# Hybrid RWKV-7 / Hyena block on one Trainium2 core: column picks on TensorE and token mixing on VectorE in the first stage, and Hyena products on VectorE with closing banks one after the other

## Chip, core and metric

The kernel runs on 1 core of one Trainium2 chip. The metric is the device time of one execution in microseconds (us), the median of several runs. The notes below name five engines: PE (TensorE), DVE (VectorE), ACT (ScalarE), POOL (GpSimd) and SP (SyncE, which here only issues DMAs).

## What is computed

Two layers over 256 latent tokens (and 256 context tokens in layer 0), width 1024, all in float32. Layer 0 mixes tokens by a bidirectional RWKV-7, layer 1 by an order-2 Hyena; each is followed by a mixture of 32 experts, top 2. Cut to what the change touches:

```python
# layer 0, the inputs of the RWKV mixer, for latent and context tokens
hx = rms_norm(x, g) * (1.0 + sc1x) + sh1x        # sc, sh: columns of cond @ ada_w + ada_b
xx = 0.5 * (prev(hx) + next(hx)) - hx
xr, xw, xk, xv, xa, xg = (hx + xx * mix[n] for n in range(6))
# low-rank products: tanh(xw @ w1), xa @ a1, sigmoid(xg @ g1)

# layer 1, Hyena: two long convolutions by Fourier products, then a projection
def _fft_conv(u, kern, skip):
    y = irfft(rfft(u) * rfft(kern))[:, :L]
    return y + u * skip
z = x1 * _fft_conv(v, kern[:, 0], skip[0])
y = x2 * _fft_conv(z, kern[:, 1], skip[1])
ox = y @ w_out + b_out
x = x + g1x * ox
```

## The kernel before

The kernel is a sequence of blocks with a barrier of all engines between them: `rwkv_inputs`, `rwkv_heads`, experts of layer 0, `hyena_inputs`, `hyena_convolutions`, experts of layer 1, `final_norm`. Inside a block each engine follows its own list in program order, and semaphores tie the lists together. The change touches the first block and `hyena_convolutions`.

**`rwkv_inputs`.** Channels lie on partitions, in 8 tiles `t` (KT = 8); `hT` holds the transposed normalized tokens (context and latent side by side, 2 x 256 columns for each tile) and `xx` the shifted difference. `FirstModulation` computes shift and scale: `products` sums cond x ada_w in one PSUM bank as the 8 weight tiles arrive, `add_bias` (L179, DVE) writes the result as a row, `columns` (L151) turns that row into columns by partition with 8 small DMAs that ACT issues, and `wait_columns` makes DVE wait for all of them. Then DVE forms `sc` and `edge` (L474 to L477), and a loop over the 8 tiles scales `hT` on DVE (L484) and `xx` on ACT (L397) and signals `tile_ready`. PE follows it tile by tile with the products for `w` (L426, L427), and after them those for `a` (L432) and `g` (L437, L439). The mixed tokens come from `mix_tokens` (L345): DVE forms a, g, k and r, 8 instructions each, with one signal `mixed` at the end of each name; POOL forms v with 8 multiplications (L503) and 8 additions (L506).

**`hyena_convolutions`.** For each of two orders `od`: PE transposes `u` and applies the forward transform to half 0 of the channels, then half 1 (L2643), ACT copies the spectra out as `vhat` (L2682). DVE forms the real part of the product with the filter spectrum (L2704, L2705, L2707), POOL the imaginary part (L2691, L2692, L2694), each in three instructions over 128x1024. PE then runs the inverse transform (L2654) over the 8 channel tiles `m`; for each half it waits for both parts before its first product. DVE closes each `m` with three instructions: `u * skip` (L2712), the transform times norm plus that (L2714), and the gate (L2717 or L2719). After order 1 PE multiplies by `w_out` (L2666) into four PSUM banks, with `m` outside and the banks inside, so that all four end in the last `m`; DVE adds bias, multiplies by the gate row and adds to `x_res`, three instructions for each bank (L2728, L2730, L2732). SP waits for `y_done` 8 (the end of the inverse transform of order 1) before it loads the first `up` and `down` weights of layer 1's experts.

**What follows.** The experts of layer 1 load 16 pairs of experts through rings of buffers; each load waits until PE has finished with the buffer.

Of the kernel before, what the change touches and what calls it, by code (L numbers as in the profile page):

```python
# [17 lines left out]
ALU = mybir.AluOpType  # L18
# [3 lines left out]
P = 128  # L22
D = 1024
L = 256
# [88 lines left out]
class FirstModulation:  # L113
# [4 lines left out]
    def __init__(self, s, ins, low, scale, shift):  # L118

        self.s, self.ins, self.scale, self.shift = s, ins, scale, shift  # L120
        self.raw, self.sig, self.cond = s.take(2, KT), s.take(2, KT), s.take(KT, 32)
        self.w = [low[:, t * FIRST:(t + 1) * FIRST] for t in range(6)] + [s.take(FIRST) for _ in range(KT - 6)]
        self.bias, self.row = s.take(512), s.take(512)
        self.cond_in, self.sig_done, self.cond_ready = s.sem("cond_in"), s.sem("cond_sig"), s.sem("cond_ready")
        self.ada_in = [s.sem(f"ada_in{t}") for t in range(KT)]
        self.bias_in, self.sum_done, self.row_ready, self.cols_in = (s.sem(n) for n in ("ada_b_in", "ada_sum", "ada_row", "ada_cols"))

    def load_conditions(self, sp):
        sp.dma_start(self.raw[:, 0], self.ins["c"].rearrange("b (p t) -> p (b t)", t=KT)).then_inc(self.cond_in, 16)
        sp.dma_start(self.raw[:, 1], self.ins["c_ctx"].rearrange("(p t) -> p t", t=KT)).then_inc(self.cond_in, 16)  # L130

# [13 lines left out]

    def columns(self, act):
        act.wait_ge(self.row_ready, 1)
        for q in range(self.PARTS):
            dst = (self.shift, self.scale)[q // 2]
            for i in range(2):  # L150
                act.dma_start(dst[q % 2 * 64:q % 2 * 64 + 64, 1 - i, :],  # L151
                              self.row[q * 32 + i:q * 32 + i + 1, :].rearrange("o (p t) -> o p t", t=KT)).then_inc(self.cols_in, 16)

    def wait_columns(self, dve):
        dve.wait_ge(self.cols_in, self.PARTS * 2 * 16)

# [12 lines left out]
    def conditions(self, dve):  # L169
        dve.memset(self.cond, 0.0)  # L170
        dve.drain()
        dve.wait_ge(self.sig_done, 1)
        dve.tensor_tensor(self.s.cond, self.raw[:, 0], self.sig[:, 0], ALU.mult)
        dve.tensor_tensor(self.cond[:, :, 0:2].rearrange("p t i -> p i t"), self.raw, self.sig, ALU.mult).then_inc(self.cond_ready, 1)
# [121 lines left out]
def rwkv_inputs(s, r, ins):  # L296
# [34 lines left out]
    def both(v):  # L331
        return v.rearrange("p (i c) -> p i c", i=2)
# [4 lines left out]
    def mix_tokens(dve, name):  # L337

        k = which[name]
        for t in range(KT):  # L340
            if name in "rg":
                args = (dst[name][:, t], xx[:, t * 2 + 1], mix[:, k, t:t + 1], hT[:, t * 2 + 1, 1:L + 1])
            else:
                args = (both(dst[name][:, t]), xx[:, t * 2:t * 2 + 2], mix[:, k, t:t + 1], inner(t))
            op = dve.scalar_tensor_tensor(*args, ALU.mult, ALU.add)  # L345
        return op

    tiles = [(ctxn, 0), (ctxn, 1), (s.x_res, 0), (s.x_res, 1)]

    with nc.Block(name="rwkv_inputs", no_gpsimd_drain=True) as block:  # L350
# [17 lines left out]
        def _(act):  # L368
# [38 lines left out]
        def _(pe):  # L407
# [6 lines left out]
            for t in turn_order:  # L414
# [14 lines left out]
            pe.wait_ge(a_in, 32)  # L429
            pe.wait_ge(mixed, 1)  # L430
            for t in range(KT):
                mm = pe.matmul(s.psum[3][:, :], a1[:, t].rearrange("p a b -> p (a b)"), xa[:, t], start=(t == 0), stop=(t == KT - 1))  # L432
            mm.then_inc(lora_done, 1)
            pe.wait_ge(g_in, 16)
            pe.wait_ge(mixed, 2)
            for t in range(KT):
                pe.matmul(s.psum[4][:, 0:L], g1[:, t, 0:P], xg[:, t], start=(t == 0), stop=(t == KT - 1))  # L437
            for t in range(KT):
# [4 lines left out]
        def _(dve):  # L443
# [29 lines left out]
            first.wait_columns(dve)  # L473
            dve.tensor_scalar(sc, sc, 1.0, None, ALU.add)  # L474
            dve.tensor_scalar(edge, sh.rearrange("p i t -> p t i"), -0.5, None, ALU.mult)
            dve.drain()
            dve.tensor_tensor(sc, sc, ng.unsqueeze(1).to_broadcast([P, 2, KT]), ALU.mult)  # L477
            dve.drain()
            dve.sem_inc(scale_ready, 1)
            ends = xx.rearrange("p a b -> p a b")  # L480
            for t in range(KT):
# [7 lines left out]
                dve.sem_inc(tile_ready, 1)  # L489
            for name in ("a", "g", "k", "r"):  # L490
                mix_tokens(dve, name).then_inc(mixed, 1)

        @block.gpsimd
        def _(pool):
# [4 lines left out]
            pool.sem_inc(folded, 1)  # L499
            pool.wait_ge(tile_ready, KT)  # L500
            to = lambda t: both(r.xv[:, t])
# [5 lines left out]
            pool.drain()  # L507

# [1769 lines left out]
def hyena_layer(s, hy, experts, ins, mods):  # L2278
# [66 lines left out]
    with nc.Block(name="hyena_inputs", no_gpsimd_drain=True) as block:  # L2345
# [263 lines left out]
        ("vT_done", "vt_ready", "dft_done", "vhat_ready", "real_ready", "imag_ready", "y_done", "y_ready"))  # L2609
    o_done = S("o_done")  # L2610
    with nc.Block(name="hyena_convolutions", no_gpsimd_drain=True) as block:
# [15 lines left out]
        def _(pe):  # L2627
            for od in range(2):
# [17 lines left out]

                for m in range(CH):
                    if m % 4 == 0:
                        pe.wait_ge(real_ready, od * 2 + m // 4 + 1)
                        pe.wait_ge(imag_ready, od * 2 + m // 4 + 1)  # L2650
                    k = 0
                    for part in range(2):
                        for ft in range(2):
                            mm = pe.matmul(s.psum[m // 2][:, m % 2 * L:(m % 2 + 1) * L], prod[:, part, ft, m * P:(m + 1) * P], inv[part][:, ft],  # L2654
                                           start=(k == 0), stop=(k == 3))
                            k += 1
                    if m % 2:
                        mm.then_inc(y_done, 1)
            pe.wait_ge(vhat_ready, 16)
            for m in range(CH):  # L2660
                pe.wait_ge(y_ready, 9 + m)
                if m % 4 == 0:
                    pe.wait_ge(wout_in[m // 4], 16)
                for i in range(TT):
                    for h in range(2):
                        mm = pe.matmul(s.psum[4 + i * 2 + h][:, :], u[:, CH + m, i * P:(i + 1) * P], w_out[:, m, h * 512:(h + 1) * 512],  # L2666
                                       start=(m == 0), stop=(m == CH - 1))
                        if m == CH - 1:
                            mm.then_inc(o_done, 1)

        @block.scalar
        def _(act):
            for od in range(2):
                for half in range(2):
# [9 lines left out]
        @block.gpsimd  # L2684
        def _(pool):

            for od in range(2):
                for half in range(2):
                    c = slice(half * 512, (half + 1) * 512)
                    pool.wait_ge(vhat_ready, (od * 2 + half) * 4 + 4)  # L2690
                    pool.tensor_tensor(prod[:, 1, :, c], vhat[:, 0, :, c], khat[:, od, 1, :, c], ALU.mult)  # L2691
                    pool.tensor_tensor(half_b, vhat[:, 1, :, c], khat[:, od, 0, :, c], ALU.mult)  # L2692
                    pool.drain()
                    pool.tensor_tensor(prod[:, 1, :, c], prod[:, 1, :, c], half_b, ALU.add).then_inc(imag_ready, 1)  # L2694
                    pool.drain()

        @block.vector
        def _(dve):
            for od in range(2):

                for half in range(2):
# [4 lines left out]
                    dve.drain()  # L2706
                    dve.tensor_tensor(prod[:, 0, :, c], prod[:, 0, :, c], half_a, ALU.subtract).then_inc(real_ready, 1)  # L2707
                    dve.drain()

                for m in range(CH):  # L2710
                    dve.wait_ge(y_done, od * 4 + m // 2 + 1)
                    dve.tensor_scalar(u[:, m], u[:, m], skip[:, od * CH + m:od * CH + m + 1], None, ALU.mult)  # L2712
                    dve.drain()
                    dve.scalar_tensor_tensor(u[:, m], s.psum[m // 2][:, m % 2 * L:(m % 2 + 1) * L], norm[:, od * CH + m:od * CH + m + 1], u[:, m], ALU.mult, ALU.add)  # L2714
# [99 lines left out]
```

## Time and profile before

| quantity | value |
|---|---|
| runs | 2031.36, 2028.88, 2026.99 us; median 2028.88 |
| profiled execution | 2029.0 us, its span 2027.2 us |
| mean granted TensorE clock | 0.949 |
| PE, DVE, ACT, POOL busy | 88%, 39%, 26%, 9% of the span |
| `rwkv_inputs` | from 0 to about 81.4 us |
| `hyena_convolutions` | from about 1402.5 to 1512.4 us |

All positions below are us from the start of the span. The shares of busy time are means over stages with different limits; what a change inside one block is worth is read from the chain of waits inside that block, and then from whether the blocks behind it start their own work relative to its end.

### The profile page before, as it was taken

The page shows a single profiled execution, that of the slowest core. Times are in us where ns is not written, and L with a number is a line of the kernel's source. Part 1 is how long each engine was busy: PE and PEld are TensorE (multiplying, and loading weights), DVE is VectorE, ACT ScalarE, POOL GpSimd, SP SyncE. Part 2 cuts the span into 40 slices and gives each one's busy share as a digit, 9 for nine tenths or more (in the row PEclk, how much of TensorE's full clock was granted, in tenths as well). Part 3 has the DMA queues.
Part 4 walks back from the last instruction along what each step waited for, and adds up shares of the span by engine and source line. Part 5 has one row for each costly group of instructions (what it writes and reads, how often), then busy time and mean ns, then how long its engine had stood idle before and what let it go on. Part 6 is the DMA issues. An engine that isn't in the chain of part 4 may idle for free. (4 is left out here: it accounts for less than half of the span.)

```text
span 2027.2 us, 34188 instructions
## 1 busy us (share of the span) xinstructions
PE 1778.4 (88%) x13907; PEld 951.2 (47%) x13907; DVE 787.7 (39%) x1857; ACT 534.6 (26%) x985; POOL 179.2 (9%) x121
## 2 busy tenths in 40 slices
PE   3868888887887897999999999798887999999996
PEld 1435545455545545444344443575545434443442
DVE  4766675666676534411011000574844301100101
ACT  2244543544544412111111111313111111111111
POOL 1512102102112000000000000000600000000000
PEclk8879998999989897999999999899997999999998
DMA  9012322323323447999999998233154999999993
GB/s 298 0 57 80 99 84 84 104 80 100 102 82 101 155 137 314 423 428 429 428 428 428 429 428 313 84 125 119 69 221 190 422 428 428 428 428 429 429 410 126
DMA packets 105808, 504.06 MB, mean 249 GB/s; under 512 B 16208, under 2 KB 60992, under 8 KB 79824
## 3 DMA queue, kind: packets, MB, share of 16 engines
q1 hardware_dynamic: 103728, 501.88, 62.4%
q8 instruction: 90, 1.47, 0.3%
q10 hardware_dynamic: 1952, 0.39, 0.1%
q14 instruction: 38, 0.31, 0.0%
HBM read 501.13 MB, written 1.09 MB: 248 GB/s over the span
## 5 line engine op out<-in xcount | busy, mean ns | idle before, releaser
L2005 DVE TENSOR_TENSOR arena<-banks,arena 128x512 f32<-128x512 f32 x32 | 22.1, 692 | 661.0 <-PE banks L1820 661.0
L1820 PE MATMUL banks<-arena 128*64 128x512 f32 x1024 | 226.3, 594 | 11.1 <-DMA arena<-in_moe_w_up 11.1
L1842 PE MATMUL banks<-arena 128*64 128x512 f32 x1024 | 226.8, 595 | 3.3 <-ACT arena L1936 3.3
L1811 PE MATMUL banks<-arena 128*64 128x512 f32 x1024 | 225.3, 592 | 3.3 <-DVE arena L1928 3.3
L800 PE MATMUL banks<-arena 128*128 128x512 f32 (+1 forms) x384 | 158.6, 550 | 0.8 <-ACT arena L1109 0.8
L1820 PEld LDWEIGHTS banks<-arena 128*64 128x64 f32 x1024 | 82.1, 137 | 153.7 <-issue 153.7
L1811 PEld LDWEIGHTS banks<-arena 128*64 128x64 f32 x1024 | 74.3, 137 | 147.8 <-issue 144.2
L1842 PEld LDWEIGHTS banks<-arena 128*64 128x64 f32 x1024 | 70.7, 137 | 154.5 <-issue 150.7
L1930 ACT ACTIVATE arena<-banks,arena 128x128 f32<-128x128 f32 x128 | 48.2, 457 | 341.4 <-PE banks L1800 341.4
L1800 PEld LDWEIGHTS banks<-arena 128*128 128x128 f32 x1024 | 121.8, 199 | 28.1 <-issue 24.3
L1800 PE MATMUL banks<-arena 128*128 128x128 f32 x1024 | 127.9, 285 | 3.5 <-DVE arena L2000 3.5
L1849 PE MATMUL banks<-arena 128*128 128x512 f32 x256 | 115.4, 593 | 2.4 <-ACT arena L1941 2.4
L2194 POOL TENSOR_TENSOR x_res<-x_res,arena 128x512 f32<-128x512 f32 x8 | 9.9, 1263 | 1106.0 <-DVEq L2170 566.5
L800 PEld LDWEIGHTS banks<-arena 128*128 128x128 f32 x384 | 69.5, 194 | 60.1 <-issue 51.1
L1940 ACT ACTIVATE arena<-banks 128x512 f32<-128x512 f32 x32 | 19.1, 597 | 282.5 <-PE banks L1842 282.5
L2424 PE MATMUL banks<-arena 128*128 128x256 f32 x384 | 87.4, 386 | 0.0
L1928 DVE TENSOR_SCALAR arena<-banks,arena 128x128 f32<-128x128 f32 x128 | 43.7, 403 | 100.8 <-PE banks L1800 100.8
L2424 PEld LDWEIGHTS banks<-arena 128*128 128x128 f32 x384 | 73.4, 193 | 17.0 <-issue 6.9
L1849 PEld LDWEIGHTS banks<-arena 128*128 128x128 f32 x256 | 46.1, 190 | 50.0 <-issue 45.9
L228 PE MATMUL banks<-arena 128*32 128x384 f32 (+1 forms) x384 | 50.0, 595 | 16.8 <-DMA arena<-in_ada_w 12.2
L1921 ACT ACTIVATE arena<-banks 128x512 f32<-128x512 f32 x32 | 19.1, 597 | 169.7 <-PE banks L1811 169.7
L737 POOL TENSOR_TENSOR arena<-arena,const 128x512 f32<-128x512 f32 x16 | 20.4, 1276 | 435.4 <-PE banks L911 421.0
(393 smaller groups left out, 2550.2 us busy)
## 6 DMA issues: line engine op xcount, KB each, us to landing
arena<-in_moe_w_gate SPq DMA_DIRECT2D x64, 2048.0 KB, 14.9
arena<-in_moe_w_up SPq DMA_DIRECT2D x64, 2048.0 KB, 17.1
arena<-in_moe_w_down SPq DMA_DIRECT2D x64, 2048.0 KB, 13.5
arena<-in_ada_w SPq DMA_DIRECT2D x128, 192.0 KB, 2.9
arena<-in_ada_w SPq DMA_DIRECT2D x64, 256.0 KB, 3.5
arena<-in_rw_wrkv SPq DMA_DIRECT2D x24, 512.0 KB, 5.1
arena<-in_hy_w_in SPq DMA_DIRECT2D x6, 2048.0 KB, 8.8
arena<-in_ada_w SPq DMA_DIRECT2D x8, 1024.0 KB, 17.1
```

The costliest lines, as they stand in the source:

```text
L228: mm = pe.matmul(bank[g * 32:(g + 1) * 32, 0:self.width(piece)], self.cond[:, half * self.HALF + g], self.w[g][:, 0:self.width(piece)], st ...
L737: pool.tensor_tensor(M1, src, mask("lev1", BLK), ALU.mult)
L800: mm = pe.matmul(s.psum[OPEN.bank(n, name)][:, 0:width], wkv[k][:, t], x[:, t], start=(t == 0), stop=(t == KT - 1))
L1800: mm = pe.matmul((X0, X1)[k // 4][:, k % 4 * P:(k % 4 + 1) * P], hx[:, t, k * P:(k + 1) * P], sel[par][:, t].rearrange("p a b -> p (a b)") ...
L1811: mm = pe.matmul(G[j * CAP:(j + 1) * CAP, :], xT[:, t, j * CAP:(j + 1) * CAP], wg[par][j][:, t], start=(t == 0), stop=(t == KT - 1))
L1820: mm = pe.matmul(U[j * CAP:(j + 1) * CAP, :], xT[:, t, j * CAP:(j + 1) * CAP], wu[j][:, t], start=(t == 0), stop=(t == KT - 1))
L1842: mm = pe.matmul(bank[j * CAP:(j + 1) * CAP, :], hT[:, t, j * CAP:(j + 1) * CAP], wd[j][:, t, half * 512:(half + 1) * 512], start=(t == 0) ...
L1849: pe.matmul(OUT[k][:, :], selwT[par][:, k // 2], y[:, k % 2 * 512:(k % 2 + 1) * 512], start=start, stop=stop).then_inc(scat_done, 1)
L1928: op = eng.tensor_scalar(xT[:, k], src, sc[:, k:k + 1], sh[:, k:k + 1], ALU.mult, ALU.add)
L1930: op = eng.activation(xT[:, k], src, ACT.Identity, bias=sh[:, k:k + 1], scale=sc[:, k:k + 1])
L2005: dve.tensor_tensor(h, U[:, :], sg, ALU.mult).then_inc(h_ready, 1)
L2424: mm = pe.matmul(s.psum[n % 2][:, 0:L], win_ring[k][:, t, q * P:(q + 1) * P], hT[:, t], start=(t == 0), stop=(t == KT - 1))
```

## The change

In the first block the shift and scale columns come from TensorE: 16 products with columns of the identity pick the row's entries into partitions (bank 5), and DVE reads them from PSUM. The context's condition takes slot 0 and the latent's slot 1, so that the columns come out in order. The last difference on `xx` is split into three quarters, `add_bias`, and one quarter. POOL's mixing for v goes to DVE, between k and r, and every mixing instruction signals `mixed`, so that PE takes `a` and `g` by the tile.

In `hyena_convolutions` DVE forms both parts of the products and POOL nothing. The inverse transform runs by half, then by part, so that the real part's products need only `real_ready`. `u * skip` goes to ACT. The output projection runs `m` = 0 to 3 as before and then bank by bank over `m` = 4 to 7, each bank with its own `o_done`.

```diff
+    def columns(self, pe, bank):
+        pick = self.s.c("ident").rearrange("p (a h r) -> p h a r", a=2, h=2)
+        pe.wait_ge(self.row_ready, 1)
+        for t in range(KT):
+            for h in range(2):
+                mm = pe.matmul(bank[h * 64:(h + 1) * 64, t * 4:(t + 1) * 4], self.row[:, t::KT], pick[:, h, :, 0:2], start=True, stop=True)
+        mm.then_inc(self.cols_done, 1)
+    def take_columns(self, dve, bank, gain, edge):
+        cols = bank[:, 0:KT * 4].rearrange("p (t a i) -> p t a i", a=2, i=2)
+        dve.wait_ge(self.cols_done, 1)
+        dve.scalar_tensor_tensor(self.scale.rearrange("p i t -> p t i"), cols[:, :, 1], 1.0,
+                                 gain.unsqueeze(2).to_broadcast([P, KT, 2]), ALU.add, ALU.mult)
+        dve.tensor_copy(self.shift.rearrange("p i t -> p t i"), cols[:, :, 0])
+        dve.tensor_scalar(edge, cols[:, :, 0], -0.5, None, ALU.mult)
...
-            first.columns(act)
...
             first.products(pe, s.psum[0], range(2, KT))
+            pe.wait_ge(raw_act, 3)
+            first.columns(pe, s.psum[5])
...
-            first.add_bias(dve, s.psum[0])
-            dve.scalar_tensor_tensor(xx, xx, 0.5, hT[:, :, 1:L + 1], ALU.mult, ALU.subtract)
+            for at in (slice(0, 3 * KT // 2), slice(3 * KT // 2, 2 * KT)):
+                if at.start:
+                    first.add_bias(dve, s.psum[0])
+                dve.scalar_tensor_tensor(xx[:, at], xx[:, at], 0.5, hT[:, at, 1:L + 1], ALU.mult, ALU.subtract)
...
-            for name in ("a", "g", "k", "r"):
-                mix_tokens(dve, name).then_inc(mixed, 1)
+            for name in ("a", "g", "k", "v", "r"):
+                mix_tokens(dve, name)
...
-            for t in range(KT):
-                pool.tensor_scalar(to(t), xx[:, t * 2:t * 2 + 2], mix[:, which["v"], t:t + 1], None, ALU.mult)
-            pool.drain()
-            for t in range(KT):
-                pool.tensor_tensor(to(t), to(t), inner(t), ALU.add)
...
+                for half in range(2):
                     for part in range(2):
+                        pe.wait_ge((real_ready, imag_ready)[part], od * 2 + half + 1)
+                        for m in range(4 * half, 4 * half + 4):
+                            for ft in range(2):
+                                mm = pe.matmul(...)
+                            if part == 1 and m % 2:
+                                mm.then_inc(y_done, 1)
...
+            for k in range(4):
+                for m in range(CH // 2, CH):
+                    if k == 0:
+                        pe.wait_ge(y_ready, 9 + m)
+                    mm = out_product(m, k)
+                mm.then_inc(o_done, 1)
...
+                for m in range(CH):
+                    act.activation(u[:, m], u[:, m], ACT.Copy, scale=skip[:, od * CH + m:od * CH + m + 1]).then_inc(skip_ready, 1)
...
                     dve.tensor_tensor(prod[:, 0, :, c], prod[:, 0, :, c], half_a, ALU.subtract).then_inc(real_ready, 1)
+                    dve.tensor_tensor(prod[:, 1, :, c], vhat[:, 0, :, c], khat[:, od, 1, :, c], ALU.mult)
+                    dve.tensor_tensor(half_b, vhat[:, 1, :, c], khat[:, od, 0, :, c], ALU.mult)
+                    dve.drain()
+                    dve.tensor_tensor(prod[:, 1, :, c], prod[:, 1, :, c], half_b, ALU.add).then_inc(imag_ready, 1)
...
-                    dve.tensor_scalar(u[:, m], u[:, m], skip[:, od * CH + m:od * CH + m + 1], None, ALU.mult)
-                    dve.drain()
+                    dve.wait_ge(skip_ready, od * CH + m + 1)
```

## Rows read from the trace of the kernel before

**Rows 1.** Page, busy us, share of the span and instructions.

```profile
PE 1778.4 (88%) x13907; PEld 951.2 (47%) x13907; DVE 787.7 (39%) x1857; ACT 534.6 (26%) x985; POOL 179.2 (9%) x121
```

**Rows 2.** Windows: length, then busy us of each engine, clock, DMA share, GB/s.

```profile
1510.00:1560.00 50.00, 37.61 (x181) 28.33 (x182) 21.87 (x97) 13.93 (x22) 0.00 (x0) 0.69 0.38 150
1600.00:1700.00 100.00, 98.71 (x486) 42.31 (x484) 8.45 (x21) 16.10 (x32) 0.00 (x0) 1.00 1.01 427
```

**Rows 3.** Timeline of PE late in layer 1's experts: start, length, instruction, wait.

```profile
1900.54 7.09 PE L1820 MATMUL banks<-arena 128*64 128x512 f32 x32 [0.49 <-DMA arena<-in_moe_w_up]
...
1929.91 7.09 PE L1820 MATMUL banks<-arena 128*64 128x512 f32 x32 [0.50 <-DMA arena<-in_moe_w_up]
```

**Rows 4.** Timeline of the first block and the start of the second.

```profile
27.58 4.42 DVE L466 TENSOR_TENSOR arena<-arena 128x4096 f32<-128x4096 f32 x1
...
34.16 0.69 DVE L179 TENSOR_TENSOR arena<-banks,arena 128x512 f32<-128x512 f32 x1 [2.16 <-PE banks L163]
...
45.38 0.17 DVE L474 TENSOR_SCALAR arena<-arena 128x16 f32<-128x16 f32 x1 [6.20 <-DMA arena<-arena]
...
46.01 6.49 ACT L397 ACTIVATE arena<-arena 128x256 f32<-128x256 f32 x16 [19.06 <-DVEq L478]
...
47.30 2.05 PE L426 MATMUL banks<-arena 128*128 128x512 f32 x2 [13.28 <-DVEq L488]
...
53.80 27.57 DVE L345 SCALAR_TENSOR_TENSOR arena<-arena 128x512 f32<-128x512 f32 x32
...
76.58 0.38 ACT L403 ACTIVATE arena<-banks 128x256 f32<-128x256 f32 x1 [5.14 <-PE banks L439]
...
83.81 2.08 PE L791 MATMUL banks<-arena 64*128 64x512 f32 x4 [7.27 <-DVEq L1541]
```

**Rows 5.** Line L345 in 54.5 to 56, and in 80.3 to 81.4: ns min/median/max.

```profile
L345 DVE SCALAR_TENSOR_TENSOR arena<-arena x3: 741/750/1096, 53.8 to 55.5; 128x512 f32<-128x512 f32 x3
...
L345 DVE SCALAR_TENSOR_TENSOR arena<-arena x2: 470/470/471, 80.5 to 80.9; 128x256 f32<-128x256 f32 x2
```

**Rows 6.** Timeline of the Hyena products, order 0.

```profile
1414.66 1.23 DVE L2704 TENSOR_TENSOR arena<-arena 128x1024 f32<-128x1024 f32 x1 [12.48 <-ACT arena L2682]
...
1415.80 3.37 DVE L2705 TENSOR_TENSOR arena<-arena 128x1024 f32<-128x1024 f32 x1
...
1423.46 2.29 DVE L2704 TENSOR_TENSOR arena<-arena 128x1024 f32<-128x1024 f32 x1 [0.99 <-ACT arena L2682]
1424.81 8.83 PE L2654 MATMUL banks<-arena 128*128 128x256 f32 x32 [2.02 <-POOL arena L2694]
...
1434.67 7.14 PE L2654 MATMUL banks<-arena 128*128 128x256 f32 x32 [1.03 <-POOL arena L2694]
1434.75 0.48 DVE L2714 SCALAR_TENSOR_TENSOR arena<-banks,arena 128x256 f32<-128x256 f32 x1
1435.31 0.42 DVE L2717 TENSOR_TENSOR arena<-arena 128x256 f32<-128x256 f32 x1
1435.65 0.35 DVE L2712 TENSOR_SCALAR arena<-arena 128x256 f32<-128x256 f32 x1
```

**Rows 7.** Timeline of order 1's end, the projection, and the next block.

```profile
1461.38 7.14 PE L2654 MATMUL banks<-arena 128*128 128x256 f32 x32 [2.02 <-POOL arena L2694]
...
1471.24 7.14 PE L2654 MATMUL banks<-arena 128*128 128x256 f32 x32 [2.72 <-POOL arena L2694]
...
1478.22 27.63 PE L2666 MATMUL banks<-arena 128*128 128x512 f32 x64
...
1503.39 0.69 DVE L2728 TENSOR_TENSOR arena<-banks,arena 128x512 f32<-128x512 f32 x1 [21.82 <-PE banks L2666]
...
1512.74 3.65 PE L1858 MATMUL banks<-const,x_res 128*128 128x128 f32 x16 [6.89 <-PEq L2611]
```

**Rows 8.** Timeline: the same router product in layer 0 and in layer 1.

```profile
773.89 1.95 PE L1864 MATMUL banks<-arena 128*128 128x36 f32 x16 [0.46 <-DVE arena L2026]
...
1516.64 3.60 PE L1864 MATMUL banks<-arena 128*128 128x36 f32 x16 [0.25 <-DVE arena L2026]
```

More of the change, by code:

```diff
@@ L125, in __init__ @@
         self.ada_in = [s.sem(f"ada_in{t}") for t in range(KT)]
[L126 removed]
+        self.bias_in, self.sum_done, self.row_ready, self.cols_done = (s.sem(n) for n in ("ada_b_in", "ada_sum", "ada_row", "ada_cols"))
     def load_conditions(self, sp):
[L129 to L130 removed]
+        sp.dma_start(self.raw[:, 1], self.ins["c"].rearrange("b (p t) -> p (b t)", t=KT)).then_inc(self.cond_in, 16)
+        sp.dma_start(self.raw[:, 0], self.ins["c_ctx"].rearrange("(p t) -> p t", t=KT)).then_inc(self.cond_in, 16)
     def load_bias(self, act):
@@ L144, in sigmoid @@
         act.activation(self.sig, self.raw, ACT.Sigmoid).then_inc(self.sig_done, 1)
[L146 to L155, printed above, removed]
+    def columns(self, pe, bank):
[12 more added lines that the diff above has]
+        dve.tensor_scalar(edge, cols[:, :, 0], -0.5, None, ALU.mult)
     def products(self, pe, bank, tiles):
@@ L344, in mix_tokens @@
                 args = (both(dst[name][:, t]), xx[:, t * 2:t * 2 + 2], mix[:, k, t:t + 1], inner(t))
-            op = dve.scalar_tensor_tensor(*args, ALU.mult, ALU.add)
-        return op
+            dve.scalar_tensor_tensor(*args, ALU.mult, ALU.add).then_inc(mixed, 1)
     tiles = [(ctxn, 0), (ctxn, 1), (s.x_res, 0), (s.x_res, 1)]
@@ L429, in _ @@
             pe.wait_ge(a_in, 32)
-            pe.wait_ge(mixed, 1)
             for t in range(KT):
+                pe.wait_ge(mixed, t + 1)
                 mm = pe.matmul(s.psum[3][:, :], a1[:, t].rearrange("p a b -> p (a b)"), xa[:, t], start=(t == 0), stop=(t == KT - 1))
@@ L434, in _ @@
             pe.wait_ge(g_in, 16)
-            pe.wait_ge(mixed, 2)
             for t in range(KT):
+                pe.wait_ge(mixed, KT + t + 1)
                 pe.matmul(s.psum[4][:, 0:L], g1[:, t, 0:P], xg[:, t], start=(t == 0), stop=(t == KT - 1))
@@ L472, in _ @@
             dve.wait_ge(vec_in, 2 * 16)
-            first.wait_columns(dve)
-            dve.tensor_scalar(sc, sc, 1.0, None, ALU.add)
-            dve.tensor_scalar(edge, sh.rearrange("p i t -> p t i"), -0.5, None, ALU.mult)
-            dve.drain()
-            dve.tensor_tensor(sc, sc, ng.unsqueeze(1).to_broadcast([P, 2, KT]), ALU.mult)
+            first.take_columns(dve, s.psum[5], ng, edge)
             dve.drain()
@@ L2609, in hyena_layer @@
         ("vT_done", "vt_ready", "dft_done", "vhat_ready", "real_ready", "imag_ready", "y_done", "y_ready"))
-    o_done = S("o_done")
+    o_done, skip_ready = S("o_done"), S("skip_ready")
     with nc.Block(name="hyena_convolutions", no_gpsimd_drain=True) as block:
@@ L2645, in _ @@
                         mm.then_inc(dft_done, 1)
[L2647 to L2651, printed above, removed]
-                    for part in range(2):
[L2653 to L2658, printed above, removed]
+                for half in range(2):
+                    for part in range(2):
+                        pe.wait_ge((real_ready, imag_ready)[part], od * 2 + half + 1)
+                        for m in range(4 * half, 4 * half + 4):
+                            for ft in range(2):
+                                mm = pe.matmul(s.psum[m // 2][:, m % 2 * L:(m % 2 + 1) * L], prod[:, part, ft, m * P:(m + 1) * P], inv[part][:, ft],
+                                               start=(m % 2 == 0 and part == 0 and ft == 0), stop=(m % 2 == 1 and part == 1 and ft == 1))
+                            if part == 1 and m % 2:
+                                mm.then_inc(y_done, 1)
@@ L2659, in _, with out_product @@
+            def out_product(m, k):
+                i, h = divmod(k, 2)
+                return pe.matmul(s.psum[4 + k][:, :], u[:, CH + m, i * P:(i + 1) * P], w_out[:, m, h * 512:(h + 1) * 512],
+                                 start=(m == 0), stop=(m == CH - 1))
             pe.wait_ge(vhat_ready, 16)
-            for m in range(CH):
+            for m in range(CH // 2):
                 pe.wait_ge(y_ready, 9 + m)
[L2662 to L2669, printed above, removed]
+                if m == 0:
+                    pe.wait_ge(wout_in[0], 16)
+                for k in range(4):
+                    out_product(m, k)
@@ L2671, in _ @@
+            pe.wait_ge(wout_in[1], 16)
+            for k in range(4):
+                for m in range(CH // 2, CH):
[3 more added lines that the diff above has]
+                mm.then_inc(o_done, 1)
         @block.scalar
```

17 lines of the change are left out of this document (1 added, 16 removed).

## The prediction

> **What bounds the kernel now.** I read the page first. TensorE is busy 88% of the span and VectorE 39% [rows 1], so on average neither of the touched engines (VectorE, GpSimd) is the limit, and a change to them can only pay inside the two blocks it edits, where barriers make a late engine everybody's. So the second thing to ask is whether the blocks behind pass a shift on. The windows show the experts of layer 1 with PE at 98.7% and the DMA engines full at 427 GB/s [rows 2], and late in them PE waits a little at every pair for the `up` weights, at a period of 1929.91 - 1900.54 = 29.37 us [rows 3]: that is the weight stream's period. It is a stream that PE starts: each load waits for a buffer that PE frees, and in 1510 to 1560 the DMA engines are busy only 38% of the time [rows 2], which is some 31 us of slack in front of it. An earlier end of `hyena_convolutions` should therefore arrive at the end of the kernel in full. The heads block, too, starts its loads and products relative to its own barrier, so the same is expected of the first block.
>
> Third, the timeline of the two blocks. In the first the row of shift and scale is there at 34.85, and VectorE goes on only at 45.38, after a wait for the column DMAs [rows 4]. The tile loop runs 46.01 to 53.80. Then VectorE mixes for 27.57 us and ends the block at 81.37; TensorE and ScalarE are through at about 77.2 (L403 at 76.58, and the short one behind it), so VectorE closes the block by 4 us [rows 4]. In the Hyena block TensorE waits for GpSimd's imaginary part in front of each of the four halves: 2.02, 1.03, 2.02, 2.72 us [rows 6, 7].
>
> **What mixing and products cost without GpSimd.** The 128x1024 product takes 1.23 us when it starts ahead of GpSimd's, and 3.37 us for the next of the same shape, with GpSimd's beside it [rows 6]. L345 shows the same: 128x512 takes 741 ns at the best and 1096 at the worst within 1.5 us, and 128x256 takes 470 ns once GpSimd is done [rows 5]. So the two engines hold each other up, and the sum uses the low values. For a pitch from start to start: L466 has 4096 elements in 4.42 us, and the two last 256-element instructions start 0.40 apart (80.5 to 80.9) [rows 4, 5]. A line through both gives 1.04 ns for an element and 0.13 us fixed, so 0.67 us for 512; the product of 1024 has a pitch of 1.14 (1414.66 to 1415.80) [rows 6].
>
> The Trainium skill (SBUF — State Buffer, section on the two separate sides) says that VectorE, when it reads two SBUF inputs, and GpSimd take one port pair as an exclusive lock for a whole instruction, and that the loser blocks. By that rule the long values are waiting and not work, which agrees with the 1.23 beside 3.37; without it the slow rival below would have to get a larger chance. The trace shows it only where both engines run, and only for two or three instructions the free price.
>
> **First block, part by part.** (1) L466 ends at 32.0. Three quarters of the difference are 3072 elements, 3.3 us, to 35.4; then `add_bias`, 0.69, to 36.1. That is 1.3 us later than before, because `sum_done` at about 34.0 now waits behind the 3.3 us. (2) The picks: 16 products, which the trace will show as 32, as it does for float32. Not in the trace before. Nearest is L1864, 16 instructions with 128-column weights and 36 moving columns in 1.95 us at full clock and 3.60 at half [rows 8], so 0.11 and 0.22 each. The picks have 64 columns of weights: below, half of 0.11, so 1.8 us in all; above, the whole 0.22, so 7 us. TensorE has then been idle for 2 us and may be at either clock; I take 3.0. (3) `take_columns` and drains, 0.8 us, against 0.6 before. Tile loop from about 40.0 in place of 46.0: 6.0 earlier. (4) Tile loop unchanged, 7.8 us, to 47.9. (5) VectorE mixes 24 of 512 and 16 of 256: 24 x 0.67 + 16 x 0.40 = 22.5 us, to 70.4. (6) TensorE and ScalarE: from the first L426 at 47.30 to the end of ScalarE at 77.2 is 29.9 us of products that wait only for tiles that come in time (`a` is mixed by 53.3, needed at about 56.5; `g` by 56.5, needed at 63.4). Moved to 41.3 they end at 71.2. So TensorE is the next to be late: the block ends at 71.2 and not at 70.4, and the gain is 81.4 - 71.2 = 10.1 us. Taking a and g by the tile costs and gains nothing, since TensorE is still in the `w` products; if that cover were gone the wait would be 5 us. The column DMAs leave ACT's queue, behind which nothing but the scaling stood. The 40 signals are not in the trace: I take nothing for them; even 0.02 us each would stay in the 0.8 us that VectorE is ahead.
>
> **Hyena block.** Half 0 of order 0: VectorE from 1414.66, six instructions and two drains at 1.14 to 1.23, real part ready at 1418.3, imaginary at 1421.9. Half 1's spectra come at 1423.4 [rows 6]: real at 1427.1, imaginary at 1430.8 (before: 1434.5). TensorE ends its forward transforms at 1422.8 and goes straight on: 32 instructions at 0.217 are 6.95 us, to 1429.7, half 1's real part to 1433.1 and the imaginary to 1436.6; nothing is waited for, with 2.4 us to spare at the tightest place. Before it was 1434.67 + 6.9 = 1441.6. Of the 5.0 us, 2.0 and 1.0 are the waits, 1.7 the clock dip in 8.83 against 7.14 [rows 6], the rest the gap. Order 1: the same waits again, 2.0 and 2.7, together 4.7 [rows 7], and no dip to save; sum 9.7, and with rounding of ends 9.9. `u * skip` on ScalarE: 8 x 0.41 (L397: 16 in 6.49 us) behind its last copy, done at 1426.8, 4 us before VectorE asks; if that cover were gone it would cost 3.3 us per order. Closings: per `m` 0.56 + 0.34 = 0.90 us in place of 0.90 + 0.42 [rows 6]; they are covered by TensorE's next transforms before as after.
>
> Projection: the same 64 instructions, 27.6 us, from 1468.3 to 1495.9. Before, the first bank came 24.9 us into it and VectorE needed four times three instructions, to 1512.37 [rows 7]; now three banks are closed while TensorE works and the last takes 0.1 + 0.76 + 0.76 + 0.69 = 2.3 us, to 1498.1. After TensorE's end 6.5 us become 2.3: 4.3 less. Sum of the block: 9.9 + 4.3 = 14.2 us. The first `up` and `down` loads leave 10 us earlier, the next gate loads 14 us earlier; PE wants them some 50 us after, so they cost nothing.
>
> **Sum.** 10.1 + 14.2 = 24.3 us. There is also the clock: TensorE starts the heads block and the router after shorter idle times (3 us in place of 7.27 and 2.7 in place of 6.89 [rows 4, 7]). The three router products in a row would take 1.95 in place of 3.60 each, up to 4.8 us [rows 8]; in the heads block 2.08 + 9.30 us of products at mostly half clock hide up to 2.7. Idle times of 2 to 3 us in this trace were sometimes followed by the half clock (the 8.83) and sometimes not (7.14 after 2.02 and 2.72 us of waiting) [rows 6, 7]. I count 1 us of these 7.5. So the profiled 2029.0 (span 2027.2, and 1.8 around it) becomes 2029.0 - 25.3 = 2003.7. The median of the runs, 2028.88, is the same number within 0.1.
>
> **Rivals.**
> - The clock stays up in both places: 2029.0 - 24.3 - 7.5 = 1997.2. For it, the shorter idle; against it, the 8.83. Chance 0.15 for more than half of it.
> - A new wait in the first block: picks at the upper bound (7 us), 4 later, or TensorE colder in the `w` products. 2008 to 2010. Chance 0.12.
> - Part of the gain is absorbed: the weight stream of layer 1 cannot start earlier, and Hyena's 14.2 are lost, 2018; or the heads block loses the 10.1, 2014. Against it, the 38% [rows 2]. Chance 0.06.
> - The other sign: the 3.3 us are VectorE's own price for such a product and 1.23 the exception. Then 12 products in a row for each order take 39.6 us: order 0 ends at 1414.66 + 39.6 + 3.5 = 1457.8, 16.3 later than before, both orders 32 later, less 4.3; the first block mixes 27.57 + 8 x 1.01 = 35.7 us and ends at 83.5, 2 later. Together 30 slower, 2059. It starts to be slower than before where the product costs over 2.5 us: 2 x (12p - 23.3) = 14.4. Chance 0.03.
> - It does not do what it says: no engine is freed because TensorE is the bound in both blocks anyway; 2025 to 2033. Against it the four waits for POOL. Chance 0.03.
>
> The forecast has the remaining 0.61 (2001 to 2008). The range that leaves out two in ten reaches into the clock's case and over the first block's: 1997 to 2011. A measurement of this kernel can tell some 0.2%, 4 us: faster by more 0.94, within 0.03, slower 0.03.
>
> **What would show it.** Right: L2704 to L2707 and the three behind them all at 1.15 to 1.25 us; TensorE without a wait over 0.3 us in front of the inverse transforms; `w_out` products from about 1458 (1468 less the first block's 10); L345 at 0.74 and 0.47, 40 of them; the first L426 about 6 us earlier; the block's last work on ScalarE. Wrong: a wait of VectorE for `skip_ready`; L345 over 0.9 us; picks that last over 5 us; waits for `in_moe_w_up` that appear in the first pairs of layer 1.

## The result, and the profile after

The changed kernel takes 2001.05 us (median of 4 runs, 1998.48 to 2007.12) against 2027.93 for the kernel before (4 runs, 2024.94 to 2031.36); ratio 0.987, 95% interval 0.9846 to 0.9895. By that ratio it is 26.4 us less (21 to 31); between the two medians it is 26.9. The forecast was 2003.7 from 2029.0, 25.3 less. The profiled execution is the slowest of the four, 2007.12 with a span of 2005.2 us, so it shows only 22.0 us of the gain; where the rest lies is a question of its own below.

The page's engine line, beside [rows 1]: GpSimd's 68.6 us have gone, and VectorE, which took over that work, is busy 18 us less.

```profile
PE 1776.6 (89%) x13939; PEld 949.0 (47%) x13939; DVE 769.8 (38%) x1862; ACT 541.1 (27%) x1001; POOL 110.6 (6%) x93
```

The timeline of the first block, beside [rows 4]:

```profile
32.01 3.36 DVE L477 SCALAR_TENSOR_TENSOR arena<-arena 128x3072 f32<-128x3072 f32 x1
...
35.28 0.68 DVE L185 TENSOR_TENSOR arena<-banks,arena 128x512 f32<-128x512 f32 x1
35.41 1.90 POOL L501 TENSOR_TENSOR arena<-arena 128x1024 f32<-128x1024 f32 x1 [35.00 <-DMA arena<-in_rw_w]
...
35.88 2.51 DVE L477 SCALAR_TENSOR_TENSOR arena<-arena 128x1024 f32<-128x1024 f32 x1
...
36.11 2.09 PE L152 MATMUL banks<-const,arena 128*64 128x4 f32 x32 [2.07 <-DVE arena L185]
...
38.58 0.18 DVE L158 SCALAR_TENSOR_TENSOR arena<-banks,arena 128x16 f32<-128x16 f32 x1 [0.19 <-issue]
...
40.33 2.05 PE L432 MATMUL banks<-arena 128*128 128x512 f32 x2 [2.12 <-DVEq L492]
...
57.17 3.17 PE L438 MATMUL banks<-arena 128*128 128x512 f32 x7
...
71.26 0.38 ACT L407 ACTIVATE arena<-banks 128x256 f32<-128x256 f32 x1 [5.14 <-PE banks L445]
...
72.31 0.17 DVE L1527 MEMSET arena<- 128x128 f32 x1 [3.15 <-PEq L355]
...
74.29 2.08 PE L787 MATMUL banks<-arena 64*128 64x512 f32 x4 [3.07 <-DVEq L1537]
```

The wait for the column DMAs is gone: VectorE takes the columns at 38.58 where it stood until 45.38. VectorE is idle for 3.15 us before the barrier, so TensorE and ScalarE now end the block, and the next block's first product starts at 74.29 in place of 83.81.

The timeline of the Hyena products, beside [rows 6]. GpSimd is absent, each product takes 1.22 or 1.23 us, and one row of 64 instructions on TensorE has taken the place of two with waits between them:

```profile
1411.12 1.22 DVE L2695 TENSOR_TENSOR arena<-arena 128x1024 f32<-128x1024 f32 x1 [11.54 <-ACT arena L2684]
...
1412.26 1.22 DVE L2696 TENSOR_TENSOR arena<-arena 128x1024 f32<-128x1024 f32 x1
...
1419.09 13.98 PE L2648 MATMUL banks<-arena 128*128 128x256 f32 x64
...
1419.92 1.23 DVE L2695 TENSOR_TENSOR arena<-arena 128x1024 f32<-128x1024 f32 x1 [1.57 <-ACT arena L2684]
...
1425.92 1.23 DVE L2702 TENSOR_TENSOR arena<-arena 128x1024 f32<-128x1024 f32 x1
```

The projection and the block's end, beside [rows 7]. Three banks close inside the projection; after the last one VectorE has one bank left, and TensorE's idle time in front of the router is 2.63 us in place of 6.89:

```profile
1464.26 27.63 PE L2655 MATMUL banks<-arena 128*128 128x512 f32 x64
...
1481.70 0.69 DVE L2722 TENSOR_TENSOR arena<-banks,arena 128x512 f32<-128x512 f32 x1 [15.29 <-PE banks L2655]
...
1491.93 0.69 DVE L2722 TENSOR_TENSOR arena<-banks,arena 128x512 f32<-128x512 f32 x1 [1.21 <-PE banks L2655]
...
1494.52 2.03 PE L1854 MATMUL banks<-const,x_res 128*128 128x128 f32 x16 [2.63 <-PEq L2607]
```

Later the experts of layer 1 wait for the `up` weights at the same period as before [rows 3]: 1937.34 - 1907.97 = 29.37 us.

### The profile page after: what moved, and what is told of

Read it like the earlier page. It is cut to its first block and busy times, and to the rows that moved or that the text cites. A ratio compares the mean times of both kernels' runs of the same rounds, so it can differ in the third digit from the quotient of the medians.

```text
span 2005.2 us, 34229 instructions
## 1 busy us (share of the span) xinstructions
PE 1776.6 (89%) x13939; PEld 949.0 (47%) x13939; DVE 769.8 (38%) x1862; ACT 541.1 (27%) x1001; POOL 110.6 (6%) x93
## 5 line engine op out<-in xcount | busy, mean ns | idle before, releaser
L1807 PEld LDWEIGHTS banks<-arena 128*64 128x64 f32 x1024 | 74.3, 137 | 147.8 <-issue 144.2
L898 PE MATMUL banks<-arena 64*64 64x64 f32 x512 | 24.3, 262 | 34.5 <-DVE arena L1501 20.1
```

Of the source, the lines that this page charges most:

```text
L898: mm = pe.matmul(bank[rows(z), o:o + C], PR[rows(z), 1, h, j - HALF, part * C:(part + 1) * C], V2[rows(z), j, h * C:(h + 1) * C], start=Tr ...
L1807: mm = pe.matmul(G[j * CAP:(j + 1) * CAP, :], xT[:, t, j * CAP:(j + 1) * CAP], wg[par][j][:, t], start=(t == 0), stop=(t == KT - 1))
```

## The experiments

Six lengths were read from each profile, because stages differ in how much they vary from run to run. "First" is the start of the heads block's first product (before: 83.81). "Heads" runs from there to the start of the last output product of the heads block (before: 764.9). "Between" runs from there to the first transpose of the convolutions; it holds the end of the heads block, the experts of layer 0 and `hyena_inputs`. "Conv" runs from the first transpose of the convolutions to the router's first transpose (before: 1512.74 - 1402.55). "Router" runs from there to the first expert product of layer 1. "Rest" runs from there to the end of the span. All in us; the six add up to the span. The last column is the time of the profiled execution, not the median.

| kernel | first | heads | between | conv | router | rest | time |
|---|---|---|---|---|---|---|---|
| before, first profile | 83.8 | 681.1 | 637.6 | 110.2 | 32.1 | 482.4 | 2029.0 |
| before_again | 83.4 | 683.2 | 638.2 | 110.2 | 32.1 | 481.5 | 2030.5 |
| after, first profile | 74.3 | 686.9 | 638.8 | 94.6 | 29.9 | 480.8 | 2007.1 |
| after_again | 73.2 | 682.1 | 639.0 | 95.4 | 29.9 | 481.2 | 2002.6 |
| first_only | 73.2 | 678.6 | 640.2 | 108.9 | 32.2 | 481.0 | 2015.8 |
| hyena_only | 83.0 | 686.2 | 639.5 | 94.6 | 29.9 | 481.8 | 2017.0 |
| no_stagger | 72.5 | 685.4 | 635.7 | 99.3 | 32.2 | 481.5 | 2008.4 |
| pool_beside | 74.3 | 682.8 | 642.5 | 108.2 | 29.9 | 483.2 | 2022.8 |
| v_on_pool | 76.8 | 680.6 | 641.3 | 95.4 | 29.9 | 481.5 | 2007.5 |
| skip_on_vector | 72.8 | 681.9 | 635.6 | 95.5 | 29.9 | 480.3 | 1997.9 |
| keep_busy | 75.9 | 681.9 | 642.4 | 95.8 | 29.2 | 481.3 | 2008.3 |
| parts_together | 72.6 | 686.5 | 637.8 | 98.2 | 29.9 | 482.2 | 2009.1 |
| columns_by_dma | 79.6 | 684.9 | 637.9 | 95.7 | 29.9 | 482.0 | 2011.9 |
| by_name | 74.3 | 686.8 | 635.6 | 94.5 | 29.9 | 482.5 | 2005.4 |

### Does the heads block give part of the gain back?

In the first profile the heads block starts 9.5 us early and its last product only 3.7 early (764.9 became 761.2), though the change does not touch it. The expectation below has 2.1 and 7.4 for what are 3.7 and 5.8: 2.1 us is how much earlier the run of eight instructions that ends with that product starts (760.22 became 758.07). Theory A: its length varies from execution to execution. Theory B: the change lengthens it. `after_again` and `before_again` are the two kernels unchanged.

> The changed kernel once more, for a second profile. In its first profile the first block handed over 9.5 us early and the heads block then gave back 7.4 (its last product starts 2.1 us early). Theory A, chance: the heads block's length varies with where TensorE's clock dips fall, so in this profile it gives back another amount, somewhere between 0 and 7, and the time is 1998 to 2007. Theory B, the change itself lengthens the heads block (other queue states at its start): it gives back 7 to 8 again and the time stays at 2007. Both: Hyena's convolution block and the first block have the same lengths within 0.5 us.

> The kernel before once more, for a second profile. Theory A (varying clock dips): the heads block, from its first product at 83.81 to its last at 764.9, differs from the first profile by some us, while the first block (83.8) and the Hyena convolutions (110.2 from first product to the next block's first) stay within 0.5. Theory B (the change lengthens it): its length stays within 1 us.

`after_again`: median 2003.18 (1998.28 to 2010.3, 4 runs), before 2026.62 on the same chip, ratio 0.9878 (0.9836 to 0.9919). Its heads block took 682.1 us, 4.8 less than the same code in the first profile; `before_again` took 683.2, 2.1 more than before. Over all 14 profiles the untouched block takes 678.6 to 686.9, with the old first block in front (681.1, 683.2, 686.2) as with the new one (678.6 to 686.9). The means are the same, 683.5 us for the three profiles with the old first block and 683.5 for the eleven with the new one. Theory B falls. The stretch between the heads and the convolutions, which only `keep_busy` touches (its extra products in layer 0's router lie there), varies nearly as much: 635.6 to 642.5 us.

The part of the expectation that both theories shared, lengths within 0.5 us, held for `before_again` (83.4 and 110.2, beside 83.8 and 110.2) and not for `after_again`: its first block is 1.1 us shorter and its conv 0.9 longer than in the first profile. For the conv the rows show why. Its first eight transposes, after the same 3.08 us of waiting, ran at the full clock in the first profile (granted clock 1.00) and at half in `after_again` and in `before` (0.50), and with what follows that costs 0.8 us:

```profile
1402.55 1.94 PE L2635 MATMUL banks<-const,arena 128*128 128x128 f32 x8 [3.08 <-PEq L2345]
...
1399.95 1.07 PE L2631 MATMUL banks<-const,arena 128*128 128x128 f32 x8 [3.08 <-PEq L2341]
```

(The first row is of the kernel before, the second of the changed one.) The profiles that leave the changed block's order alone fall into two groups by this: 94.5 to 94.6 at full clock (the first profile, `hyena_only`, `by_name`) and 95.4 to 95.7 at half (`after_again`, `v_on_pool`, `skip_on_vector`, `columns_by_dma`). Why the clock differs there from one execution to the next is open. Conv lengths below are compared within a group.

Why the heads block varies is not settled. Read in 34 windows for each profile, the block's length rises with TensorE's busy time (561.5 to 567.8 us for the same instructions; correlation 0.73 over 14 profiles) and only loosely with the time at the half clock (0.52). The shortest block, `first_only`, has the highest clock (0.937), but `parts_together`, with 0.935, is among the longest.

### One half of the change at a time

`first_only` has the changed `FirstModulation` and `rwkv_inputs` and the old `hyena_layer`, `hyena_only` the reverse.

> The changed first block, Hyena as before. Prediction's sum: 10.1 us less, and by the first profile 9.5 at the start of the heads block (first product at 74.3). Theory A: the time is 2028 less 9.5, give or take 4 of clock, 2018. Theory B (heads block gives 7.4 back because of the change): 2026.

> The changed Hyena convolutions, first block as before. Prediction's sum 14.2; the first profile shows 15.6 to the next block's first product and 17.8 to the first expert product, as the router keeps the clock for part of it. So 2011 to 2013. Rival, the gain is absorbed by the weight stream: 2020 or more, with waits for the up weights in the first pairs.

`first_only`: 2017.37 (8 runs), ratio 0.9947 (0.993 to 0.9965), 10.7 us less (7 to 14). `hyena_only`: 2014.72 (5 runs), ratio 0.9927 (0.9903 to 0.9952), 14.8 us less (10 to 20), and 1.7 above the 2011 to 2013 expected. Together 25.5 us by the ratios, beside 26.4 for the whole. Between the medians the two are 9.3 and 11.9 less, 21.2 together, beside 23.4 for `after_again`, so the times alone settle the sum only to some us. The stages say it more sharply: `first_only` has the new first length and the old router, `hyena_only` the old first length and the new conv and router, each as in the whole change. Both parts arrive at the end of the kernel, and neither is seen to take anything from the other. In the first pairs of `hyena_only` TensorE waits 0.7 us in all for the `up` weights between 1500 and 1700: the weight stream absorbs nothing.

### Is GpSimd's neighbourhood the cost of a product?

```diff
+        @block.gpsimd
+        def _(pool):
+            pool.memset(spare, 0.0)
+            pool.drain()
+            for od in range(2):
+                for half in range(2):
+                    pool.wait_ge(vhat_ready, (od * 2 + half) * 4 + 4)
+                    for _ in range(3):
+                        pool.tensor_tensor(spare, spare, spare, ALU.mult)
+                        pool.drain()
```

> The changed kernel, with three 128x1024 products on GpSimd over a tile that nobody else uses, beside each of VectorE's groups of six; the outputs don't depend on it. Theory (the two engines hold each other up, whatever data they touch): the first three or four of VectorE's six go from 1.22 to about 3.3 us, six take 12 to 13 us in place of 7.3, TensorE waits 3 to 5 us before the imaginary part of half 1 in each order, block 8 us longer. Rival (the old 3.3 us came from sharing the tiles vhat and khat, or from the drains): VectorE stays at 1.22 and the block is unchanged.

`spare` is a tile of 128x1024 that nothing else uses. The block took 108.2 us, 13.7 longer than in the profiles with the same clock at its start. Its timeline, the first group of six:

```profile
1410.90 1.23 DVE L2709 TENSOR_TENSOR arena<-arena 128x1024 f32<-128x1024 f32 x1 [11.65 <-ACT arena L2687]
1410.94 8.60 POOL L2699 TENSOR_TENSOR arena<-arena 128x1024 f32<-128x1024 f32 x3 [10.42 <-ACT arena L2687]
...
1412.04 2.92 DVE L2710 TENSOR_TENSOR arena<-arena 128x1024 f32<-128x1024 f32 x1
...
1415.03 2.76 DVE L2712 TENSOR_TENSOR arena<-arena 128x1024 f32<-128x1024 f32 x1
...
1423.53 2.76 DVE L2716 TENSOR_TENSOR arena<-arena 128x1024 f32<-128x1024 f32 x1
1426.34 13.47 PE L2651 MATMUL banks<-arena 128*128 128x256 f32 x48 [3.86 <-DVE arena L2716]
```

VectorE's own code and data are those of the changed kernel, and GpSimd works on a tile that nobody else touches: five of the six products take 2.76 to 2.92 us in place of 1.22. So the price came from the neighbour, and not from the shared tiles or from VectorE's drains; GpSimd's own drains, which this run keeps, are not told apart from its products. The size was missed (8 us expected): two groups of GpSimd, 8.6 and 8.3 us, keep VectorE slow almost without a break from 1412 to 1429, and the second group of six starts 7 us late. What the Trainium skill says of the shared port pair (SBUF — State Buffer, the section on the two separate sides) agrees with this: the loser waits for whole instructions.

### Staggered banks, order of parts, place of u * skip

`no_stagger` keeps the old loop, `m` outside and the banks inside, over all 8 `m`. `parts_together` and `skip_on_vector` (which also takes the eight instructions per order out of ScalarE's list):

```diff
-                        pe.wait_ge((real_ready, imag_ready)[part], od * 2 + half + 1)
+                        if part == 0:
+                            pe.wait_ge(real_ready, od * 2 + half + 1)
+                            pe.wait_ge(imag_ready, od * 2 + half + 1)
...
-                    dve.wait_ge(skip_ready, od * CH + m + 1)
+                    dve.tensor_scalar(u[:, m], u[:, m], skip[:, od * CH + m:od * CH + m + 1], None, ALU.mult)
+                    dve.drain()
```

> The changed kernel with the output projection in the old order, all four banks ending in the last m. Expected: from the projection's end on TensorE to the next block's first product 6.9 us as before in place of 2.6, so the block is 4.3 us longer; the router's products all at half clock again, another 2 us. Rival: VectorE's tail was hidden anyway, no difference.

> The changed kernel, but TensorE waits for both parts before each half's first product, as before the change. Products of half 0 end at 1426.1 in the first profile, and half 1's imaginary part is ready at 1427.15: so TensorE waits 1.1 to 1.2 us in each order, and the convolution block is 2.3 us longer than its 94.6 to 95.5. Rival: no difference, since VectorE alone is fast enough.

> The changed kernel with u * skip on VectorE again (16 instructions of 0.35 us on its closing chain, 0.42 from start to start). Theory: closings are covered by TensorE's transposes, transforms and projection in both orders, so the block's length changes by under 0.5 us. Rival: the closings are on the path, 3.3 us for each order, 6.7 together.

All three ran with the half clock at the first transposes, so the changed kernel's 95.4 to 95.7 are what to compare with. `no_stagger`: conv 99.3, and router 32.2 against 29.9. The router's first transposes, after 6.54 us of idle TensorE, in the half-clock pace of before:

```profile
1492.87 3.44 PE L1854 MATMUL banks<-const,x_res 128*128 128x128 f32 x15 [6.54 <-PEq L2607]
```

So the staggering is worth 3.6 to 3.9 us in its block (6.54 - 2.63 = 3.91 of idle time; forecast 4.3) and 2.3 behind it. `parts_together`: conv 98.2, 2.5 to 2.8 longer (2.3 expected), with a wait of 1.14 us in front of half 1 in each order, here in order 0:

```profile
1425.14 7.14 PE L2650 MATMUL banks<-arena 128*128 128x256 f32 x32 [1.14 <-DVE arena L2704]
```

`skip_on_vector`: conv 95.5, inside the changed kernel's own spread. Its 16 extra instructions lie under TensorE's work, so moving u * skip to ScalarE is worth nothing that can be measured. Its one run took 1997.9, 4.7 us under the profiled run of `after_again`, but 3.4 of that lie in the untouched stretch between (635.6 beside 639.0).

### The parts of the first block

`v_on_pool` puts the 16 instructions for v back on GpSimd. `columns_by_dma` puts the 8 column DMAs back, with the new order of the conditions, and leaves the rest. `by_name` makes TensorE wait for all eight tiles of a and of g (the same edit at both):

```diff
-                pe.wait_ge(mixed, t + 1)
+                if t == 0:
+                    pe.wait_ge(mixed, KT)
```

> The changed kernel with v mixed on GpSimd again (8 multiplications, 8 additions beside VectorE's other four names). Theory: VectorE's 32 instructions take 27.6 us again from 46.8, to 74.4, and become the end of the block: heads block's first product at 76.8 in place of 74.3, 2.5 us later. Rival, TensorE bounds the block and VectorE's share of the change was worth nothing: no difference.

> The changed kernel with the shift and scale columns by 8 DMAs again; mixing stays on VectorE and by the tile. The row is ready at 36.0; before, the DMAs took 10.5 us from the row to VectorE's next instruction. So tiles begin at about 46.8 in place of 39.0, and the heads block's first product moves from 74.3 (72.5 to 74.3 in five profiles) to 80 to 82. Rival (the gain came from mixing on VectorE): it stays below 77.

> The changed kernel with TensorE waiting for all eight tiles of a, and of g, before the first product. a is mixed by 52.2 and g by 55.5 in the first profile, and TensorE comes to them at 57.2 and 64.0: no difference, the first block's end stays where it was (heads block's first product at 72.5 to 74.3). Rival: taking them by the tile let TensorE start earlier, 3 us or more.

`v_on_pool`: first product at 76.8, as expected, beside 72.5 to 74.3. VectorE's 32 instructions take the 27.57 us of [rows 4] to the digit, and VectorE ends the block again, with only the barrier behind it:

```profile
46.82 27.57 DVE L351 SCALAR_TENSOR_TENSOR arena<-arena 128x512 f32<-128x512 f32 x32
...
74.85 0.17 DVE L1535 MEMSET arena<- 128x128 f32 x1 [0.46 <-PEq L355]
```

The changed kernel makes 40 of them in 22.3 us (46.83 to about 69.2). `columns_by_dma`: first product at 79.6 (80 to 82 expected). VectorE waits 8.81 us for the DMAs, and the tiles begin at 45.8 (39.0 in the first profile). `by_name`: 74.3, within the spread, as expected.

### Can TensorE be kept at the full clock through the router?

```diff
+def keep_busy(s, pe, bank, n):
+    for _ in range(n):
+        pe.matmul(bank[:, :], s.c("ident"), s.const[:, 0:512], start=True, stop=True)
```

> The changed kernel with extra TensorE products that nobody reads (identity times constants, 128x512), put where TensorE waits: 2 at the first block's end, 4 behind the output projection, and in both routers 4 before the first logits, 11 before the ranks, 3 before the first gather. Theory (the router pays for the half clock that TensorE's idle time brings): from the first transpose of layer 1's router to the first expert product 24 us in place of 29.9, as 3.34 + 3.61 become 3.7, the first gather 3.84 in place of 5.70, the ranks 1 less; the like in layer 0; time 2001 less 8 to 10, 1992. Rival (those steps are bound by the chain on VectorE and the products only get in the way): the router stays within 1 us of 29.9 or grows.

2009.21 (4 runs), ratio 0.9892 (0.9866 to 0.9917), against 0.987 and 0.9878 for the changed kernel: no gain, where 8 to 10 us were expected. The timeline of PE in layer 1's router:

```profile
1501.28 1.87 PE L1866 MATMUL banks<-arena 128*128 128x36 f32 x16
1502.98 1.95 PE L1874 MATMUL banks<-arena 128*128 128x36 f32 x16
1504.77 1.95 PE L1866 MATMUL banks<-arena 128*128 128x36 f32 x16
1506.56 9.69 PE L115 MATMUL banks<-const 128*128 128x512 f32 x22
...
1519.78 3.73 PE L1802 MATMUL banks<-arena 128*128 128x128 f32 x32
```

The clock part is right: the three router products take 1.95 us or less each and the first gather 3.73 in place of 5.70. The fill was mis-sized: one extra product costs 0.86 us at the full clock (two instructions of 0.43), so 11 of them last 9.7 us where TensorE used to wait 6.0, and the four before the logits hold those back by over a microsecond. The router of layer 1 came out 0.7 us shorter, the conv, with the four behind its projection, 1.1 to 1.3 longer than in the profiles with the same clock at its start, and the first block, with its two, 1.6 to 3.4 longer. A version with about half as many was not run.

## Why the prediction was right

**Price without GpSimd.** Right. Forecast 1.14 to 1.23 us for a product and 0.67 / 0.40 us from start to start in the mixing; measured 1.22 to 1.23, and 22.3 us for the mixing against 22.5. `pool_beside` and `v_on_pool` show that it is the neighbour, so the rival with the other sign was wrong.

**First block.** Forecast 10.1 us; three profiles with the old block give 83.0 to 83.8 and eight with the new one 72.5 to 74.3, 10.0 us between the means. That this is so close is partly luck, as two terms were off in opposite directions. TensorE's first `w` product came 7.0 us earlier in the first profile (47.30 became 40.33) and 8.0 in `after_again` (39.33), where 6.0 were forecast; 0.9 of that is the picks, which took 2.09 us and not 3.0. The chain of TensorE and ScalarE from there to the block's end was put at its old 29.9 us and took 31.6 (40.33 to 71.90). In the old profile the `w` products had begun at half clock for about 3 us (granted clock 0.55 from 47.30 to 50.4), in the new one for over 6 (0.53 from 40.33 to 46.8), so they took 16.8 us and not 15.2. The second profile of the kernel before has 16.6 for them (46.91 to 63.47), unseen because VectorE ended that block: the forecast had taken its length from the quicker of two. This is the rival "TensorE colder in the `w` products", which came in part.

A step that the sum did not have stood beside the picks: the last quarter of the difference took 2.51 us in place of 1.2, because GpSimd's 1.90 us began at 35.41, just ahead of it, so it ended at 38.4, together with the picks. That TensorE and ScalarE would be the next to end, and not VectorE, was right. What the split of the difference is worth was not tried by itself.

**What the columns and the mixing are worth each.** `columns_by_dma` loses 5.3 to 7.1 us, `v_on_pool` 2.5 to 4.3: together about the whole gain. By the tile is worth nothing, as forecast.

**Hyena block.** Forecast 14.2. At half clock in the first transposes the block took 110.2 us before (two profiles) and 95.4 to 95.7 after (four), 14.5 to 14.8 less; at full clock 108.9 (`first_only`) and 94.5 to 94.6 (three), 14.2 to 14.4 less. From its first transpose to the projection, 75.67 us in `before` became 65.21 in `after_again`, both at half clock: 10.5 less where 9.9 were forecast (of which 0.2 were called rounding and not worked out). In the first profile it is 64.31, and the further 0.9 is the clock of the first transposes (2.63 us to the first transform, or 1.80). The tail after TensorE's last product is 4.3 us shorter, as forecast. The part order, counted inside the 9.9, is worth 2.5 to 2.8 by `parts_together`. One sign did not come: the projection was to begin at about 1458 and began at 1464.26 in the first profile, because the heads block took 5.8 us longer there and the stretch behind it 1.2.

**Passing on.** Right: the rest behind layer 1's router is 480.3 to 483.2 us in every profile, old or new, and the two untouched stretches behind the first block have the same means with the old one (683.5 and 638.4) as with the new one (683.5 and, without `keep_busy`, 638.4).

**The clock.** This term was too small: 1 us of a possible 7.5 was counted. Layer 1's router gives 2.2 us in every profile with staggered banks (2.9 in `keep_busy`), not quite half of the 4.8 that its three products could give. In the first profile the first of the three ran at the full clock (granted 1.00) and the next fell to half: 1.9 us come from these two and 0.3 from the first gather. At the start of the heads block little came of it (8.82 us for the 16 instructions against 9.30).

Sum of the stages that the change touches: 10.0 + 14.5 + 2.2 = 26.7, against 26.4 (21 to 31) measured and 25.3 forecast. The time's own spread is too wide to tell these three apart.

## What to carry to other kernels

Before splitting elementwise work over VectorE and GpSimd, look for the price of the same instruction with and without its neighbour: here 1.23 against 3.37 us, and one engine alone did both halves sooner than the two together. Where several PSUM banks are closed by another engine, let them end one after the other; the last bank's tail is all that should stand between two stages, and behind the shorter idle time the first router product ran at the full clock in every profile (1.95 us or less in place of 3.60). And before reading a difference of a few microseconds from one profile, see how far an untouched stage moves between profiles: here 8 us of 680 and 7 of 640. Make the stages add up to the whole, or such a stretch stays out of sight.

## What the runs showed of the hardware that was not expected

The heads block, with the same instructions in all 14 profiles, took 678.6 to 686.9 us. The clock at the start of the convolutions was full in six profiles and half in eight after the same 3.08 us of waiting. And the order in which the two engines begin decides who waits: GpSimd's 128x1024 product took 1.90 us when it began 0.47 us ahead of VectorE's, whose 1024 elements then took 2.51; in `columns_by_dma` VectorE began 0.1 us ahead, took 1.22, and GpSimd's took 2.87:

```profile
35.16 1.22 DVE L470 SCALAR_TENSOR_TENSOR arena<-arena 128x1024 f32<-128x1024 f32 x1
35.26 2.87 POOL L498 TENSOR_TENSOR arena<-arena 128x1024 f32<-128x1024 f32 x1 [34.85 <-DMA arena<-in_rw_w]
```

Of the eight profiles with the new first block, GpSimd began first in three (the first, `pool_beside`, `by_name`), and the heads block started at 74.3; VectorE began first in the other five, and it started at 72.5 to 73.2. The order is not all of that: in those five VectorE's first part of the difference had also begun 0.7 to 1.2 us earlier (30.83 to 31.28 in place of 31.97 to 32.01).
